# Cross attention's scores and weighing as three float32r products of split operands

## The reference

```python
def memory_cross_attention(h, m, w_q, w_kv, w_o):
    q = (h @ w_q).reshape(Bn, S, X_HEADS, X_HEAD_DIM)
    k, v = jnp.split(m @ w_kv, 2, axis=-1)
    ...
    s = jnp.einsum('bshd,bmhd->bhsm', q, k).astype(jnp.float32) * (X_HEAD_DIM ** -0.5)
    p = jax.nn.softmax(s, axis=-1).astype(v.dtype)
    o = jnp.einsum('bhsm,bmhd->bshd', p, v).reshape(Bn, S, D_MODEL)
    return o @ w_o
```

## Time and profile before

| What | us |
|---|---|
| median of three runs | 1382.82 |
| lowest and highest | 1382.62, 1384.26 |
| profiled execution, its own time | 1384.48 |
| its span in the profile | 1382.7 |

### The profile page before, as it was taken

One profiled execution on the slowest core, in us unless ns is written; L12 is line 12 of the kernel. 1 busy time (PEld: TensorE's weight loads), 2 busy tenths in 40 slices (PEclk: granted clock), 3 DMA queues, 4 the chain that ended last, 5 costly groups with the idle time before them and its releaser, 6 DMA issues.

```text
span 1382.7 us, 18120 instructions
## 1 busy us (share of the span) xinstructions
PE 1370.2 (99%) x7261; PEld 1158.4 (84%) x7261; DVE 890.4 (64%) x1037; ACT 742.0 (54%) x984; POOL 150.8 (11%) x251
## 2 busy tenths in 40 slices
PE   8999999999999999999999999999999999999998
PEld 7988888888888888877788888888888877788886
DVE  5986657656567666665876566666666646676663
ACT  6647555444455444465765444554444667554443
POOL 1000101111011111110211110021170100000000
PEclk9999999999999999999999999999999999999999
DMA  9953345756648556554357666585655644365550
GB/s 295 311 183 130 133 164 163 241 189 203 201 139 265 188 190 199 179 189 139 127 168 230 194 201 199 168 238 191 193 192 169 204 147 137 117 233 185 194 170 31
DMA packets 121363, 255.38 MB, mean 185 GB/s; under 512 B 6394, under 2 KB 32830, under 8 KB 121279
## 3 DMA queue, kind: packets, MB, share of 16 engines
q1 hardware_dynamic: 117036, 250.99, 55.5%
q0 software_dynamic: 4096, 3.15, 0.9%
q10 hardware_dynamic: 146, 0.07, 0.0%
HBM read 253.14 MB, written 1.05 MB: 184 GB/s over the span
## 4 chain that ended last, share of the span: by engine, by line
PE 98%; ACT 1%; DVE 0%; issue 0%; DMA 0%; POOL 0%; DVEq 0%; ACTq 0%; POOLq 0%
PE ps L1654 20%; PE ps L1364 18%; PE ps L1366 18%; PE ps L1365 18%; PE ps L1657 10%; PE ps L1352 1%; PE ps L1354 1%; PE ps L1353 1%; PE ps L1387 1%; PE ps L1377 1%; PE ps L1424 1%; PE ps L1469 1%; PE ps L1631 1%; PE ps L1397 1%; PE ps L1692 1%; PE ps L1451 0%
## 5 line engine op out<-in xcount | busy, mean ns | idle before, releaser
L972 DVE TENSOR_TENSOR w_lo<-raw,w_hi 128x2048 fp32r<-128x2048 f32 x225 | 516.8, 2301 | 275.2 <-ACT w_hi L679 273.9
L679 ACT CAST w_hi<-raw 128x2048 fp32r<-128x2048 f32 x225 | 428.2, 1910 | 210.0 <-PE ps L1366 136.5
L1654 PE MATMUL ps<-hT,w_hi 128*128 128x512 f32 x1216 | 304.4, 392 | 0.1
L1654 PEld LDWEIGHTS ps<-hT,w_hi 128*128 128x128 f32 x1216 | 220.0, 189 | 40.5 <-issue 0.3
L1364 PE MATMUL ps<-w_hi,yT_hi 128*128 128x512 f32 x640 | 252.9, 395 | 0.7 <-DVE yT_lo L1232 0.7
L1366 PE MATMUL ps<-w_hi,yT_lo 128*128 128x512 f32 x640 | 249.5, 390 | 0.0
L1365 PE MATMUL ps<-w_lo,yT_hi 128*128 128x512 f32 x640 | 249.4, 390 | 0.0
L1364 PE MATMUL ps<-w_hi,hT 128*128 128x512 f32 (+1 forms) x496 | 193.8, 391 | 0.0
L1366 PE MATMUL ps<-w_hi,hT 128*128 128x512 f32 (+1 forms) x496 | 188.6, 380 | 0.0
L1365 PE MATMUL ps<-w_lo,hT 128*128 128x512 f32 (+1 forms) x496 | 188.2, 379 | 0.0
L1657 PEld LDWEIGHTS ps<-hT,w_lo 128*128 128x128 f32 x1216 | 165.9, 190 | 11.9
(11 more groups left out here) (196 smaller groups left out, 1256.9 us busy)
## 6 DMA issues: line engine op xcount, KB each, us to landing
raw<-ffn_wd SPq DMA_DIRECT2D x44, 1024.0 KB, 5.3
raw<-ffn_wg SPq DMA_DIRECT2D x40, 1024.0 KB, 6.0
raw<-ffn_wu SPq DMA_DIRECT2D x40, 1024.0 KB, 5.4
raw<-w_ff SPq DMA_DIRECT2D x32, 1024.0 KB, 5.9
raw<-diff_w_in SPq DMA_DIRECT2D x12, 1024.0 KB, 5.2
raw<-na_w_in SPq DMA_DIRECT2D x12, 1024.0 KB, 5.2
raw<-w_in SPq DMA_DIRECT2D x10, 1024.0 KB, 6.4
raw<-w_xkv SPq DMA_DIRECT2D x8, 1024.0 KB, 11.3
```

The costliest lines, as they stand in the source:

```text
L679: act.copy(hi_part(c), raw[:, c % NRAW, :]).then_inc(hi_done, 1)
L972: dve.tensor_tensor(lo_part(c), raw[:, c % NRAW, :], hi_part(c), ALU.subtract).then_inc(lo_done, 1)
L1654: pe.matmul(ps[:, 4 + j, :], wh[:, i, j * P:j * P + P], h_both[:, 4 * last + i, :, :], start=first and i == 0, stop=False)
```

## The change

ScalarE's copies of the turned q and of the turned probabilities now write float32r (`xq_hi`, `xp_hi`, in the places of `qT` and `probT`), and VectorE gets the difference to PSUM as `xq_lo` and `xp_lo`. Two new words in the plan, `ks` and `vs`, split mem's keys and values whole: ScalarE copies 128x2048 elements to float32r, VectorE subtracts in place. TensorE makes three float32r products where there was one plain one, and waits for the low parts. VectorE now acts on the words `tq` (`turned_q_lo`) and Q (`turned_prob_lo`) of the cross stage too. The first product of the output projection also waits for `xq_low`. No load is added or removed.

```diff
-    "cross": ("qa0.0 add1 s qb0.0 gain1 s sq1 rq0.0 qc0.0 turn1 qd0.0 tq0.0 rq1.0 qa0.1 s qb0.1 tq1.0 rq0.1 s qc0.1 "
+    "cross": ("qa0.0 add1 s qb0.0 gain1 s sq1 rq0.0 qc0.0 turn1 qd0.0 tq0.0 rq1.0 qa0.1 s ks qb0.1 tq1.0 rq0.1 s vs qc0.1 "
               "tq0.1 h qd0.1 rq1.1 exp " +
...
+        xp_lo = nc.alloc_sbuf_tensor_at("xp_lo", [P, TT, D], F32R, offset=nc.sbuf_base - 4 * TT * D)[:, :, 512:1024]
...
+        def rounded(name, shape):
+            return nc.alloc_sbuf_tensor_at(name, shape, F32R, offset=nc.sbuf_base - 4 * int(np.prod(shape[1:])))
...
         qT = sb("qT", [P, KT, S])
+        xq_hi = rounded("xq_hi", [P, KT, S])
         kT = sb("kT", [P, KT, S])
+        km_hi = rounded("km_hi", [P, KT, S])
         vv = sb("vv", [P, TT, D])
+        vm_hi = rounded("vm_hi", [P, TT, D])
         big = sb("big", [P, 3 * CH])
+        big_lo = rounded("big_lo", [P, 3 * CH])
+        km_lo = big_lo[:, 0:CH].rearrange("p (k s) -> p k s", k=KT)
+        vm_lo = big_lo[:, CH:2 * CH].rearrange("p (t d) -> p t d", t=TT)
+        xq_lo = big_lo[:, 2 * CH:3 * CH].rearrange("p (k s) -> p k s", k=KT)
...
         probT = sb("probT", [P, 2, 512])
+        xp_hi = rounded("xp_hi", [P, 2, 512])
...
+                    to = xp_hi if kind == "cross" else probT
+                    act.copy(to[:, b, 0:n], ps[:, PT_BANK, 0:n]).then_inc(pt_ready, 1)
...
+                if name == "ks":
+                    act.wait_ge(s_ready, 8)
+                    act.copy(km_hi[:, :, :], kmT).then_inc(mem_high, 1)
+                if name == "vs":
+                    act.wait_ge(o_ready, 8)
+                    act.wait_ge(m_ready, 8)
+                    act.copy(vm_hi[:, :, :], vm).then_inc(mem_high, 1)
...
-                        dst = qT if letter == "q" else kT
+                        dst = xq_hi if kind == "cross" else qT if letter == "q" else kT
...
+                def turned_prob_lo(u):
+                    dve.wait_ge(pt_ready, u0 + u + 1)
+                    dve.tensor_tensor(xp_lo[:, u % 2, :], ps[:, PT_BANK, :], xp_hi[:, u % 2, :], ALU.subtract).then_inc(xp_low, 1)
...
+            def mem_lo(name):
+                dve.wait_ge(mem_high, 1 if name == "ks" else 2)
+                to, hi, src = (km_lo, km_hi, kmT) if name == "ks" else (vm_lo, vm_hi, vm)
+                dve.tensor_tensor(to, src, hi[:, :, :], ALU.subtract).then_inc(mem_low, 1)
+
+            def turned_q_lo(word):
+                nb = word.digit
+                g, count = group_at("cross", "q", nb)
+                for t in range(TT) if word.half is None else (word.half,):
+                    part = (slice(None), slice(4 * nb, 4 * nb + 4), slice(t * P, (t + 1) * P))
+                    dve.wait_ge(qk_evac[t], count)
+                    dve.tensor_tensor(xq_lo[part], group_bank(g, t).rearrange("p (k s) -> p k s", k=4), xq_hi[part],
+                                      ALU.subtract).then_inc(xq_low[t], 1)
...
-                                ins = pe.matmul(o, qT[:, 2 * s + i, t * P:(t + 1) * P], kmT[:, 2 * s + i, :],
-                                                start=(i == 0), stop=(i == 1))
+                                hi, lo = (m[:, 2 * s + i, t * P:(t + 1) * P] for m in (xq_hi, xq_lo))
+                                pe.matmul(o, hi, km_hi[:, 2 * s + i, :], start=(i == 0), stop=False)
+                                pe.matmul(o, hi, km_lo[:, 2 * s + i, :], start=False, stop=False)
+                                ins = pe.matmul(o, lo, km_hi[:, 2 * s + i, :], start=False, stop=(i == 1))
...
                     if u >= 1:
                         pe.wait_ge(pt_ready, u0 + u)
+                        if kind == "cross":
+                            pe.wait_ge(xp_low, u)
...
-                    pe.wait_ge(pt_ready, u0 + u + 1)
+                    if kind == "cross":
+                        pe.wait_ge(xp_low, u + 1)
+                        pe.wait_ge(mem_low, 2)
+                    else:
+                        pe.wait_ge(pt_ready, u0 + u + 1)
...
-                                ins = pe.matmul(o, vm[:, kt, cols], probT[:, b, 256 * kt:256 * kt + 256],
-                                                start=(kt == 0), stop=(kt == TT - 1))
+                                hi, lo = (m[:, b, 256 * kt:256 * kt + 256] for m in (xp_hi, xp_lo))
+                                pe.matmul(o, vm_hi[:, kt, cols], hi, start=(kt == 0), stop=False)
+                                pe.matmul(o, vm_hi[:, kt, cols], lo, start=False, stop=False)
+                                ins = pe.matmul(o, vm_lo[:, kt, cols], hi, start=False, stop=(kt == TT - 1))
...
+                    elif kind == "cross":
+                        pe.wait_ge(mem_low, 1)
+                        for t in range(TT):
+                            pe.wait_ge(xq_low[t], in_part + 1)
```

More of the change, by code:

```diff
@@ L370, in build @@
         lam_dot, lam_exp, lam_ready, bias_masked = sem("lam_dot"), sem("lam_exp"), sem("lam_ready"), sem("bias_masked")
+        xq_low, xp_low = [sem(f"cross_q_low_{t}") for t in range(TT)], sem("cross_probT_low")
+        mem_high, mem_low = sem("mem_keys_values_high"), sem("mem_keys_values_low")
         dve_link, act_link, pool_link = sem("dve_link"), sem("act_link"), sem("pool_link")
@@ L763, in unit_word @@
                     n = turned_at(kind, 1, 1) + P
-                    act.copy(probT[:, b, 0:n], ps[:, PT_BANK, 0:n]).then_inc(pt_ready, 1)
+                    to = xp_hi if kind == "cross" else probT
+                    act.copy(to[:, b, 0:n], ps[:, PT_BANK, 0:n]).then_inc(pt_ready, 1)
                 if part == "A":
@@ L1232, in out_lo @@
                     dve.tensor_tensor(yT[1][:, tiles, :], src, yT[0][:, tiles, :], ALU.subtract).then_inc(o_lo, 1)
-                {"M": scores_max, "N": normalise, "B": sub_norm, "O": out_lo}[part](u)
+                def turned_prob_lo(u):
+                    dve.wait_ge(pt_ready, u0 + u + 1)
+                    dve.tensor_tensor(xp_lo[:, u % 2, :], ps[:, PT_BANK, :], xp_hi[:, u % 2, :], ALU.subtract).then_inc(xp_low, 1)
+                {"M": scores_max, "N": normalise, "B": sub_norm, "O": out_lo, "Q": turned_prob_lo}[part](u)
+            def mem_lo(name):
[10 more added lines that the diff above has]
+                                      ALU.subtract).then_inc(xq_low[t], 1)
             def rope(word):
@@ L1329, in _ @@
                         hidden_word(kind, word)
-                    elif kind in ATT and word.name in ("M", "N", "B", "O"):
+                    elif kind in ATT and (word.name in ("M", "N", "B", "O") or kind == "cross" and word.name == "Q"):
                         unit_word(kind, word.name, word.digit)
+                    elif word.name in ("ks", "vs"):
+                        mem_lo(word.name)
+                    elif kind == "cross" and word.name == "tq":
+                        turned_q_lo(word)
                     elif kind == "diff" and word.name in ("rq", "rk"):
@@ L1494, in unit_word @@
                             pe.wait_ge(qk_evac[t], max(group_at(kind, letter, in_part)[1]
-                                                       for letter in ("q" if kind == "cross" else "qk")))
+                                                       for letter in "qk"))
                 if part == "W" and kind == "moba":
@@ L1729, in ready @@
                         for half in range(TT):
+                            if kind == "cross":
+                                pe.wait_ge(xq_low[half], nb + 1)
                             pe.wait_ge((v_evac if letter == "v" else qk_evac)[half], group_at(kind, letter, nb)[1])
```

## The result

The changed kernel takes 1390.06 us (median of five runs, 1388.48 to 1390.06), against 1382.82 for the kernel before, measured beside it (five runs, 1382.62 to 1384.73): ratio 1.0041, 95% interval 1.003 to 1.0051. It is slower, by 5.7 us if one goes by the ratio. 1387.6 was predicted, within 1385.0 to 1391.0, so the median lies inside the range, 2.5 us above the number.

The account below looks back on a forecast made before the run. TensorE was taken to bound the kernel (busy 1370.2 of 1382.7 us). Its saving and three exposed waits, -2.3 + 3.36 + 1.75 + 2.0 = +4.8 us, on 1382.82 gave 1387.6, range 1385.0 to 1391.0.

Parts of the forecast that it names:

- TensorE's own work: Cross stage's four scores and four weighings: twelve float32r products take 1.44 us instead of 1.73 each, 2.3 us less in all.
- rival D: Cross stage: a float32r group costs more between the turnings than in a long row; 1389 to 1392 us, chance 0.04.
- First wait: Before unit 0's scores: q's low part queues behind the splits of mem's keys and values; +3.36 us, wholly exposed.
- Second wait: Before unit 2's scores: VectorE makes q's last low part ahead of unit 0's maximum, delaying the exponentials; +1.75 us.
- Third, two circles of 2.87: P0 to P1 and P1 to P2: VectorE's low part of turned probabilities precedes normalising; 1.00 us exposed each, +2.0.
- The hand-over of 0.2 us: Delay from another engine's finished result to TensorE's resumed records, priced from unit 2's scores behind the exponentials; 0.2 us.
- rival C: The clock falls after TensorE stands still before unit 0's scores; 1389.5 us, or 1391.8 if low for longer; chance 0.08.
- Rivals A and B: Cross stage: A, all waits hidden, 1380.5 us, chance 0.06; B, only the wait before unit 0's scores exposed, 1383.9 to 1385.8, 0.10.
- The forecast's own range: Whole kernel's median without any rival: 1386.4 to 1389.0 us, given chance 0.72.
- the wide range: Whole kernel's median, taking in upper B and most of C and D: 1385.0 to 1391.0 us.

Follow-up runs that it names:

- experiment 1: Changed kernel with the splits of mem's keys and values moved early and VectorE's part of the last weight split behind q's last low part; 1385.72 us, ratio 1.0014.
- experiment 6: Changed kernel with only the split of mem's values (vs) moved early, behind turn1; 1386.70 us in one run.
- experiment 2: Changed kernel with thirteen extra float32r matmuls of 512 columns, result unused, ahead of unit 0's scores to keep TensorE busy; 1387.35 us, ratio 1.0032.
- experiments 3: Changed kernel with VectorE's low part of the turned probabilities behind the next unit's normalising instead of ahead of it; 1389.07 us in one run.
- experiment 5: Changed kernel with mem's split early, q's last low part behind unit 0's maximum, and the probabilities' low part behind normalising; 1383.29 us, ratio 0.9993 to the kernel before.
- experiment 4: Changed kernel with VectorE's low part of q's last quarter behind unit 0's maximum instead of ahead of it; 1389.08 us in one run.

## Why the prediction was right, and by how much it was off

- **TensorE's own work, -2.3.** Right. Twelve records hold 1.44 us at full clock (experiment 1: scores at 179.97, the turning behind them at 181.41). From P3, which nobody delays, to the end of the stage there are two weighings: 21.64 us before, 21.04 after, 0.30 each, 0.29 predicted. The price from the first stage's row carried over, also between turnings, so rival D is out.
- **First wait, +3.36.** Measured 3.31. The queues rewritten by hand had q's last low part end 15.49 us behind the first turning of q (183.04 - 167.55); it ended 15.49 behind it (181.13 - 165.64), 0.15 before the scores. Experiment 6 shows that VectorE's queue is the one that counts, as the working had it.
- **Second wait.** From unit 0's scores to P0 the steps gave 183.24 to 189.94, 6.70 us. At full clock it is 6.75 (experiment 2) and in the changed kernel 8.10. What is missing is the clock, below.
- **Third, two circles of 2.87.** Measured 2.73 and 2.78, so 5.51 for 5.74, and P2 to P3 went as predicted. The hand-over of 0.2 us was a little too dear in this place: from the end of normalising (191.44 + 0.61 = 192.05) to P1 at 192.11 it is 0.06.
- **The clock: the step that failed.** I had given 0.08 to rival C, arguing that TensorE idled some 5 us at the end of the trace before the clock fell, so that 3.4 us in the middle would be safe. It fell in the changed kernel's profile, by the mean granted clock in all five timed runs (0.997 or 0.998, against 0.999 or 1.0 in every timed run of the kernel before) and in experiments 3 and 4, which keep the wait. The end of a trace is one sample, and this one was the longest: in the ten profiles of this study the clock falls between 2.0 us (the changed kernel) and 5.0 us (the kernel before) behind the last matmul, by the granted clock of the last windows. The Trainium skill (TensorE: Matmul & The Clock Gate, HAM oscillation) tells of waits between bursts of matmuls that bring the clock down, and this trace agrees: 3.15 us idle, then 0.50. Its price was 1.34 us; I had put 1.9 for unit 0's scores and the turning, which took 0.97 and 0.35 longer. The first records of unit 1's scores ran slow too, but unit 2's wait behind them anyway.
- **The sum.** Predicted 3.36 + 1.75 + 2.0 - 2.3 = 4.8; measured 5.90 = 4.56 at full clock (experiment 2) + 1.34. By stretches, what the working adds and what experiment 2 shows: up to unit 0's scores 3.36 and 3.32, from there to P0 0.88 and 0.93, to P2 1.41 and 1.18, to the end of the stage -0.87 and -0.87. So the waits and their price were right, and the forecast without a fall of the clock was 1.1 short in all. Rivals A and B, with hidden waits, are out by the profile.
- **The median.** 7.2 us above before, though the effect is 5.9. Before has three runs near 1382.7 and two near 1384.5; after has two near 1388.7 and three at 1390.06. The groups lie 1.8 and 1.4 us apart, and the medians fell on different ones; the means of the two lower groups differ by 5.9, those of the upper by 5.6. What I took for scatter between runs is the start of the kernel, below. The forecast's own range, 1386.4 to 1389.0, missed the median; the wide range held because it took in rival C, and on which group a median of five falls is luck.

## What to carry to other kernels

When a change lowers the work of the engine that bounds a kernel by adding steps on others, write out the queue of each other engine word by word up to the point where the bounding engine needs the result; a helper step that is 2 us long costs its full hold to everything queued behind it, where that queue has no gap (2.19 us in experiment 6). Put splits of data that has long been ready into stretches where their engines idle, and put what the bounding engine waits for ahead of what nobody waits for. If a long idle stretch of TensorE remains, count the low clock behind it too, or fill it: 3.15 us brought it down in all three profiles that kept it, up to 1.94 us (experiment 1) did not in the profiles here. That 1.94 is safe in every execution is not shown: behind the last matmul the fall came after 2.0 us at the earliest, and one of experiment 1's ten timed runs, 0.5 us above its like, has a mean granted clock of 0.998.

## What was not expected of the hardware

- **The clock's fall comes late.** TensorE had resumed at 181.28 before the granted clock fell (0.82 in the window 181 to 182, 0.50 from 182 to 185), 0.36 us after, and in experiments 3 and 4 it fell 0.60 and 0.96 us after. In all three it stayed at the low level for 3.4 us, though TensorE was busy throughout. In that stretch the 256-column products are 0.214 us apart, not 0.120.
- **The start is worth 1.9 us either way.** In the kernel before, the first eight products of 256 columns start at 12.38 and take 2.07 us; the next eight are 0.21 us apart, the spacing of the low clock. (The granted clock reads 1.00 there, so the level is read from the spacing alone.) In the changed kernel the same eight, from the same moment, are at the high one:

```profile
12.39 1.21 PE L1631 MATMUL ps<-hT,w_hi 128*128 128x256 f32 x8 [1.08 <-ACT hT L726]
```

The code up to there is the same. Of the ten profiles of this study the first turning of q comes between 167.3 and 167.8 in eight, and at 165.64 and 165.88 in two (the changed kernel and experiment 2). Their own times, 1388.48 and 1387.35, lie in the lower group of their kernel's runs; those of the kernel before and of experiments 1 and 5, with the later start, in the upper. Why the clock rises earlier in some executions was not tried; to compare stages, measure from an event behind the start.
- **Half a clock need not cost half.** In experiment 4 the low clock made the first two units' scores and the turning 1.55 us longer (4.92 against 3.37 in experiment 2), but P0 comes only 1.13 later than in experiment 5 (6.59 against 5.46 behind the scores), since the wait for the exponentials vanished: work stretched into a wait costs nothing.
